# Gates of the dense token tiles by scatter-add into a zeroed table, and an expert product split four and four

## The reference, cut to what matters

```python
s = einsum('thpd,hpnd->thpn', (ht @ w_q).reshape(T, 8, 2, 128), sub_keys)
vals, idx = top_k(s, 16)                       # per head, per half
cand = vals[:, :, 0, :, None] + vals[:, :, 1, None, :]
top_s, top_pos = top_k(cand.reshape(T, 8, 256), 16)
experts = i1 * 128 + i2                        # 8 heads x 16 = 128 experts a token, of 16384
gates = softmax(top_s)                         # over the 16 of a head
a = gelu(einsum('td,ted->te', x, u_tab[experts]))
y = einsum('te,ted->td', gates * a, v_tab[experts])
x = x + gate2 * rmsnorm(y)
```

## Time and profile before

| what | us |
|---|---|
| time, median of 3 runs (lowest to highest) | 2855.0 (2849.57 to 2856.36) |
| span of the profiled execution, first to last instruction | 2847.3 |
| TensorE matmul busy in it | 2774.5 (97%) |
| VectorE busy | 2158.4 (76%) |
| ScalarE busy | 1249.3 (44%) |
| GpSimd busy | 1313.3 (46%) |

### The profile page before, as it was taken

One profiled execution on the slowest core, in us unless ns is written; L12 is line 12 of the kernel. 1 busy time (PEld: TensorE's weight loads), 2 busy tenths in 40 slices (PEclk: granted clock), 3 DMA queues, 4 the chain that ended last, 5 costly groups with the idle time before them and its releaser, 6 DMA issues.

```text
span 2847.3 us, 43522 instructions
## 1 busy us (share of the span) xinstructions
PE 2774.5 (97%) x15948; PEld 2538.1 (89%) x15948; DVE 2158.4 (76%) x3708; ACT 1249.3 (44%) x2302; POOL 1313.3 (46%) x1036
## 2 busy tenths in 40 slices
PE   6998999999999999999999999999999999999998
PEld 5776778889999999999999999999998887877786
DVE  7655545887668778678989898777768878887888
ACT  4333662233357767744454544445522233332233
POOL 0002000000000000177878887777778888888884
PEclk9998999999999999999999999999999999999999
DMA  7520223225556566589898999899999999999996
GB/s 281 227 71 31 89 75 111 69 78 177 182 177 211 200 203 205 185 286 316 301 329 301 314 303 331 308 331 311 321 361 380 359 333 345 374 341 356 341 358 262
DMA packets 328417, 721.37 MB, mean 253 GB/s; under 512 B 44000, under 2 KB 159840, under 8 KB 326368
## 3 DMA queue, kind: packets, MB, share of 16 engines
q1 hardware_dynamic: 238176, 451.18, 44.9%
q0 software_dynamic: 90112, 268.76, 27.3%
HBM read 605.50 MB, written 114.30 MB: 253 GB/s over the span
## 4 chain that ended last, share of the span: by engine, by line
PE 57%; POOL 18%; issue 5%; DVE 2%; ACT 1%; DMA 1%; DVEq 0%; SPq 0%; ACTq 0%; POOLq 0%
PE mix L1434 47%; POOL picked_act L1872 9%; POOL rows L1879 9%; PE mix L116 5%; PE sps_all L1929 2%; PE sps_all L1947 1%; PE mix L1947 1%; ACT onehot L1641 1%; PE sps_all L1521 1%; DMA rows<-in_v,eidx 0%; DVE lo L106 0%; DVE onehot L1723 0%; DMA wq_raw<-in_w_q 0%; DVEq L1123 0%; ACT hi L101 0%
## 5 line engine op out<-in xcount | busy, mean ns | idle before, releaser
L1872 POOL DMA_INDIRECT picked_act<-act_early,aidx x384 | 467.0, 1216 | 1043.0 <-PE mix L1434 938.5
L1434 PE MATMUL mix<-a_hi,hi 128*128 128x320 f32 (+1 forms) x3072 | 810.1, 318 | 2.0 <-DVE lo L106 1.9
L1434 PE MATMUL mix<-a_lo,hi 128*128 128x320 f32 (+1 forms) x3072 | 808.8, 317 | 0.0
L1434 PE MATMUL mix<-a_hi,lo 128*128 128x320 f32 (+1 forms) x3072 | 808.5, 317 | 0.0
L1879 POOL DMA_INDIRECT rows<-in_v,eidx x512 | 651.3, 1272 | 166.4 <-issue 133.2
L1782 DVE SCALAR_TENSOR_TENSOR ys<-rows,coef,ys 128x1024 f32<-128x1024 f32 x504 | 633.9, 1284 | 118.6 <-DMA rows<-in_v,eidx 105.3
L106 DVE TENSOR_TENSOR lo<-raw,hi 128x1024 fp32r<-128x1024 f32 x384 | 469.2, 1222 | 301.4 <-ACT hi L101 301.0
L101 ACT ACTIVATE hi<-raw 128x1024 fp32r<-128x1024 f32 x384 | 404.8, 1054 | 358.3 <-PE mix L1947 348.3
L1434 PEld LDWEIGHTS mix<-a_hi,hi 128*128 128x128 f32 x3072 | 533.6, 188 | 3.2 <-ACT gelu L1650 2.3
L1434 PEld LDWEIGHTS mix<-a_lo,hi 128*128 128x128 f32 x3072 | 535.1, 188 | 0.0
L1434 PEld LDWEIGHTS mix<-a_hi,lo 128*128 128x128 f32 x3072 | 534.7, 188 | 0.0
(11 more groups left out here) (268 smaller groups left out, 3899.3 us busy)
## 6 DMA issues: line engine op xcount, KB each, us to landing
raw<-in_u SPq DMA_DIRECT2D x256, 512.0 KB, 4.9
raw<-in_v SPq DMA_DIRECT2D x128, 512.0 KB, 6.0
act_late<-gelu SPq DMA_DIRECT2D x128, 320.0 KB, 4.6
act_in<-act_late SPq DMA_DIRECT2D x128, 256.0 KB, 6.5
act_early<-gelu SPq DMA_DIRECT2D x128, 192.0 KB, 1.8
gate_d<-free_lo SPq DMA_DIRECT2D x19, 1024.0 KB, 8.1
gt<-gate_d SPq DMA_DIRECT2D x64, 256.0 KB
free_lo<-gate_d SPq DMA_DIRECT2D x64, 256.0 KB, 7.6
```

The lines of the kernel that those rows point to most:

```text
L1434: done = pe.matmul(dst, w, a[:, k, cols], start=first, stop=last)
L1872: pool.indirect_dma_start(out=g.picked_act[:, e:e + 1], out_offset=None, in_=act_tables[e // (EARLY * CHOSEN)], in_offset=bass.IndirectOff ...
```

## The change

It has two halves that lean on each other.

**Gates by scatter-add.** The gate products with everything around them go (`gate_turn` to `key_rounds`, `take_slots`, `compare`, `weigh`, `gates`, `load_gates`). In their place stands one table in DRAM, `act_gates` [128 steps, 128, 512 activations + 512 gates]. SP zeroes its gate half with eight DMAs of 4 MB in the retrieval. GpSimd, before its gathers, issues 4 tiles x 128 indirect DMAs that each add 128 gates to their places; a tile's next head waits until the 16 of its last head have landed. The dense stage loads activations and gates of a step with one DMA.

**Four and four.** `EARLY` becomes 4. The tiles are swapped: tiles 0 to 3 are dense, tiles 4 to 7 gathered. The first sweep does the four gathered tiles, the second the four dense ones, each with 24 matmuls of 512 columns. Top-k of tiles 0 to 2 is done with the scores, now in groups of two heads; tile 3 comes first in the later top-k, then 4 to 7. Rows still begin at step 133, with 21 in 10 steps, and then 2 a step. The order and number of GpSimd's picks and row fetches is the same.

```diff
-EARLY = 3
+EARLY = 4
+GATHERED_TILES = tuple(LATE + s if s < EARLY else DENSE + s - EARLY for s in range(GATHERED))
-HEAD_TILES = EARLY
+HEAD_TILES = DENSE - 1
-TOPK_ORDER = (1, 2, 3, 4, 0)
+TOPK_ORDER = tuple(t - HEAD_TILES for t in (HEAD_TILES, *GATHERED_TILES))
-ROW_EVERY = (5 / 12, 7 / 12)
+ROW_EVERY = (10 / 21, 1 / 2)
...
-    rows = 12 * (min(m, late) - ROWS_FROM + 1) // 5
-    return min(GATHERED * CHOSEN, rows + max(0, m - late) * 12 // 7)
+    rows = 21 * (min(m, late) - ROWS_FROM + 1) // 10
+    return min(GATHERED * CHOSEN, rows + max(0, m - late) * 2)
...
     if m < N:
-        parts = [(acc[:, 0:EARLY * P], slice(0, EARLY * P))]
+        parts = [(acc[:, 0:EARLY * P], slice(LATE * P, S))]
+    elif LATE * P <= HALF:
+        parts = [(acc[:, 0:LATE * P], slice(0, LATE * P))]
...
+    def clear_gates(j):
+        tables = g.act_gates[j * ZERO_TILES:(j + 1) * ZERO_TILES, :, DTOK:].rearrange("n p c -> p n c")
+        sp.dma_start(tables, g.zeros[:].unsqueeze(1).to_broadcast([P, ZERO_TILES, DTOK])).then_inc(g.zeros_stored, 16)
+
+    sp.wait_ge(g.zeros_ready, 1)
     for n in range(QTILES):
         if n + 2 < QTILES:
             sp.wait_ge(g.wq_lo_ready, n + 1)
             sp.dma_start(g.wq_raw[n % 2][:], i["w_q"][n + 2]).then_inc(g.wq_in[n % 2], 16)
+        if n < N // ZERO_TILES:
+            clear_gates(n)
...
+def finish_heads(g, dve, b):
...
+    dve.wait_ge(g.heads_exps, b + 1)
+    dve.tensor_reduce(norm, gates, AX, ALU.add)
+    for h in range(HEAD_GROUP * b, HEAD_GROUP * (b + 1)):
+        dve.scalar_tensor_tensor(g.sidx[:, 0:HEAD_TILES, h, :], g.chosen_r[:, h, :, :, 1], float(NKEYS), g.chosen_r[:, h, :, :, 0],
+                                 ALU.mult, ALU.add)
+    dve.drain()
+    dve.reciprocal(norm, norm)
+    for c in range(HEAD_TILES):
+        slots = g.sidx[:, c, group_heads(b), :]
+        dve.tensor_scalar(slots, slots, float(AG), g.gate_col[:, c:c + 1], ALU.mult, ALU.add)
+    dve.drain()
+    dve.tensor_tensor(gates, gates, norm.unsqueeze(3).to_broadcast([P, HEAD_TILES, HEAD_GROUP, TOPK]), ALU.mult)\
+       .then_inc(g.scatter_ready, 1)
...
+    def scatter_gates(t, head):
+        if head:
+            pool.wait_ge(g.scattered[t], 16 * TOPK * head)
+        for k in range(TOPK):
+            pool.indirect_dma_start(out=gate_table, out_offset=bass.IndirectOffsetOnAxis(ap=g.sidx[:, t, head, k:k + 1], axis=0),
+                                    in_=g.gates_d[:, t, head, k:k + 1], in_offset=None, compute_op=ALU.add)\
+                .then_inc(g.scattered[t], 16)
+
+    pool.memset(g.zeros[:], 0.0).then_inc(g.zeros_ready, 1)
+    for head in range(HEADS):
+        if head == 0:
+            pool.wait_ge(g.zeros_stored, 16 * N // ZERO_TILES)
+        if head % HEAD_GROUP == 0:
+            pool.wait_ge(g.scatter_ready, head // HEAD_GROUP + 1)
+        for t in range(HEAD_TILES):
+            scatter_gates(t, head)
+    pool.wait_ge(g.scatter_ready, HEADS // HEAD_GROUP + 1)
+    for head in range(HEADS):
+        scatter_gates(HEAD_TILES, head)
     act_complete(N - 1)
...
-        dve.tensor_tensor(pieces(g.cf[n % 2]), gates, pieces(g.act_in[n % ACTS]), ALU.mult)\
-           .then_inc(g.cf_ready, 1)
+        dve.wait_ge(g.ag_in_sem[n % ACTS], 16 * (n // ACTS + 1))
+        both = g.ag_in[n % ACTS]
+        dve.tensor_tensor(g.cf[n % 2][:], both[:, 0:DTOK], both[:, DTOK:], ALU.mult).then_inc(g.cf_ready, 1)
```

More of the change, by code:

```diff
@@ L62 @@
 TOPK_FROM, TOPK_PERIOD = 7, 40
[L65 to L73, removed]
+AG = 2 * DTOK
+ZERO_TILES = 16
+DENSE_FROM = 2 * N - 8
 DENSE_ORDER = (2, 3, 0, 1)
-GATE_PIECES = 2
 POOL_ADDS = 2
 ROWS_FROM, PICKS, BEATS = 133, 4, 4
-ROW_EVERY = (5 / 12, 7 / 12)
+ROW_EVERY = (10 / 21, 1 / 2)
 PICKS_FROM, PICKS_AHEAD = N + 0.75, 12
@@ L1227, in token_numbers @@
         dve.tensor_scalar(g.token_col[:, s:s + 1], g.token_col[:, 0:1], float(s % EARLY * P), None, ALU.add)
+    for t in range(DENSE):
+        dve.tensor_scalar(g.gate_col[:, t:t + 1], g.token_col[:, 0:1], float(DTOK + t * P), None, ALU.add)
 def topk_turn(m):
@@ L1233, in topk_turn, with stores_of, acts_stored @@
     return (x, at) if m >= TOPK_FROM and x < TOPK_TILES else (None, None)
[L1236 to L1264, removed]
-def key_step(m):
-    x, batch = gate_turn(m)
-    if m < 2 or (x is not None and (batch < 0 or gate_batch(m) == 0)):
-        return None
-    return m < N, None if x is None else onehot_buffer(gate_batch(m))
-def key_rounds(first):
-    whole = lambda m: [key_step(n) for n in range(m, m + ROUND)]
-    if first + ROUND > 2 * N or None in whole(first):
-        return 0
-    return next(n for n in range(1, 2 * N) if first + (n + 1) * ROUND > 2 * N or whole(first + n * ROUND) != whole(first))
+def stores_of(m):
+    return 1 if m < N or LATE == DENSE else 2
+def acts_stored(last, s):
+    return 16 * sum(stores_of(m) for m in range(s, last + 1, GELUS))
 def rows_by(m):
@@ L1385, in load_raw, with load_act_gates @@
     sp.dma_start(g.raw[m % RAWS][:], src).then_inc(g.raw_in[m % RAWS], 16)
[L1388 to L1399 removed]
+def load_act_gates(g, sp, n):
+    sp.dma_start(g.ag_in[n % ACTS][:], g.act_gates[n]).then_inc(g.ag_in_sem[n % ACTS], 16)
 def split_expert_hi(g, act, m):
@@ L1548, in gathered_steps @@
             if m == last_row_at(s) + (1 if s < GATHERED - 1 else -3):
+                if s == 0:
+                    for t in range(DENSE):
+                        sp.wait_ge(g.scattered[t], 16 * CHOSEN)
                 if s < GATHERED - 1:
@@ L1823, in sweeps_vector @@
         first_tiles(m)
-        x, batch = gate_turn(m - 1)
-        if x is not None and batch < 0:
-            take_slots(x)
-        elif x is not None:
-            add_gate_low(x * GATE_BATCHES + batch)
-        if gate_batch(m + 2) is not None:
-            compare(gate_batch(m + 2))
         topk_steps(m)
@@ L1953, in dense_product @@
             done.then_inc(g.tile_done, 1)
[L1955 to L1975 removed]
+    expert_product(g, pe, 1)
+    for first, last in ((2, N), (N, 2 * N)):
+        rounds = (last - first) // ROUND
+        with pe.Fori(0, rounds) as q:
+            for m in range(first, first + ROUND):
+                expert_product(g, pe, m, ROUND * q)
+        for m in range(first + rounds * ROUND, last):
+            expert_product(g, pe, m)
     dense_product(0)
```

267 lines of the change are left out of this document (87 added, 180 removed).

## The result

| | us |
|---|---|
| kernel after, median of 4 runs (lowest to highest) | 3124.85 (3120.09 to 3138.28) |
| kernel before, beside it | 2855.68 (2849.57 to 2857.01) |
| ratio, 95% interval | 1.0956 (1.093 to 1.0982) |
| span of the profiled execution after | 3118.3 |
| forecast (range) | 2948 (2815 to 3060) |

The change costs 9.6%. The direction was foreseen; the time lies 65 us above the top of the range.

A forecast was written before the change was run, and what follows sets the result against it. TensorE bounds the start, then GpSimd's gather issues, held up by VectorE: first row at 1343 + 1553 for 1010 instructions + 38.5 tail = 2934.5 us span; 7.7 around it and 6 for scatter risk give 2948 (range 2815 to 3060).

The forecast's parts named there:

- The scatters' price: GpSimd before its gathers: an adding scatter costs about a pick, 1.25 us undisturbed, 1.61 at worst, 1.40 taken.
- that margin: Before the first pick: scatters end at 1291 us against the pick's 1326, so they are hidden by 35 us only.
- Rival 2: GpSimd's scatters are late, at 1.6 us or more each or slow landings: 72 us and more, 3010 to 3050; chance 0.22.
- The fourth tile: GpSimd's last 128 scatters: tile ready at 876 us, they add 203 us after 1088 and end at 1291.
- The first sweep: TensorE's early key steps last 5.44 us, not 4.17, so the first pick comes at 1326 and first row near 1343.
- The main case: Gathers start later, scatters are in time, cadence is 1.49 to 1.60 us: 2895 to 3005 us; chance 0.53.
- The cadence: GpSimd's 1010 instructions after the first row: 1.52, 1.42 and 1.60 us each in three stretches, mean 1.538, sum 1553 us.
- Rival 1: GpSimd's gathers in steps 133 to 383 keep their pace and time falls: 2803 us at cadence 1.40; chance 0.20.
- TensorE's savings: Key steps and gate batches: 42 us from wider matmuls and 61 us from gate products, about 103 us for TensorE alone.
- Zeros: Eight DMAs of 4.19 MB in the retrieval, 12.6 us each, landed about 550: effect taken as 0, allowed 0 to 15 us.
- the sign that was named: A retrieval that ends after 640 us would mean that the DMAs writing zeros are in the way.
- Around the span: Outside the profiled execution: 7.7 us lie between the profiled span and the median run time.

The follow-up runs named there:

- Run 1: The changed kernel with all 512 scatters as plain writes instead of adds: 3508.91 us, ratio 1.2127 to the kernel before.
- s384: The changed kernel without the 128 scatters of tile 3, the other 384 adding as before: 2958.13 us, ratio 1.0204 to the kernel before.
- s0: The changed kernel with all 512 scatters left out, zeros still written: 2962.26 us, ratio 1.0211 to the kernel before.
- run 9: The changed kernel itself, unaltered, measured again on another chip: 3146.91 us, ratio 1.0914 to the kernel before.
- Run 10: As s0, but the sums of the first 256 rows lie in PSUM: 2934.57 us, ratio 1.017 to the kernel before.
- Runs 5: As s0, but VectorE adds only 8 of 1024 columns of every odd row: 2926.09 us, ratio 1.0112 to the kernel before.
- 11: As s0, but from the third row of a tile on, each adds only 8 columns: 2944.56 us, ratio 1.0204 to the kernel before.
- run 12: As Run 10, but with four gelu buffers instead of three: 2947.68 us, ratio 1.0172 to the kernel before.

## Why the prediction was wrong, point by point

**The scatters' price: the step that failed.** "For GpSimd's time the nearest is a pick: 1.25 us undisturbed, 1.61 us at worst" was the bound, and 1.40 was taken. Measured from start to start: 1.85 undisturbed, 1.946 in the mean. Run 1 shows that it is the add: the same instruction without it is issued in 0.96 us. The bound from above was made of hold-ups on a form that wasn't the form in question, so it bounded nothing. By the measured price the prediction's own sum comes out: 541.3 + 512 × 1.946 = 1537.7 for the first pick instead of 1326, 13 picks of 1.25 us later the first row at 1553.9 (measured 1553.71), and then 1010 × 1.538 + 38.5 gives 3146; the span was 3118.3. The prediction's own line "each 0.1 us costs 51 us once that margin is used" was right. With 0.55 us above the 1.40 it was the largest uncertainty by far, and the range gave it 72 us.

**Rival 2** had the mechanism, the signature ("if its first pick comes well after 1326") and what waits behind it. Its size, 3010 to 3050, is too small for the same reason, and of its two causes the first was right. Landings were not slow: 13.2 us of waiting in all.

**The fourth tile.** The prediction put its 128 scatters behind the other 384 (1088 + 203 = 1291), and that was right: in the trace GpSimd never idles between 541 and 1536 for more than its gaps and 13.2 us of landings, where the sum had 24. It is one line of work, the fourth tile's first scatter starts at 1282.2, and that the tile is ready at 876 plays no part.

**The first sweep.** Steps of 5.44 us, no gate matmuls, TensorE 600.0 of 600 us busy; where the sweep and not the scatters releases it, the first pick comes at 1339.7 and 1340.5 (s384, s0), forecast 1326; the 14 us are told under the zeros. The main case (loss of start time by moving a tile into the first sweep) holds by itself: forecast 2942 of 2855, 1.030; measured 1.021 in s0. The ratio agrees better than its terms, which is in part luck: in s0 the first row is 16 us late and the cadence 1.564, and the kernel before ran 47 us slower on that chip too.

**The cadence.** Forecast 1.52, 1.42 and 1.60, mean 1.538; measured in the changed kernel 1.46, 1.43 and 1.59, mean 1.516: 22 us too much. The order of the three stretches and the fall in each were right; why the first fell further than forecast wasn't tested. The same kernel on another chip (run 9) has 1.543, so a miss of this size is within what chips differ by. Its cause held: in the dense stage the timelines of GpSimd and VectorE of after show the same pattern as the earlier trace rows.

```profile
2604.09 1.36 POOL L1812 DMA_INDIRECT picked_act<-act_early,aidx  x1 [0.30 <-issue]
2605.75 1.27 POOL L1819 DMA_INDIRECT rows<-in_v,eidx  x1 [0.30 <-issue]
2607.33 1.43 POOL L1812 DMA_INDIRECT picked_act<-act_early,aidx  x1 [0.30 <-issue]
2609.06 0.94 POOL L1819 DMA_INDIRECT rows<-in_v,eidx  x1 [0.30 <-issue]
```

```profile
2604.92 1.28 DVE L1731 SCALAR_TENSOR_TENSOR ys<-rows,coef,ys 128x1024 f32<-128x1024 f32 x1 [0.29 <-DMA rows<-in_v,eidx]
2606.12 0.68 DVE L1754 TENSOR_TENSOR cf<-ag_in 128x512 f32<-128x512 f32 x1
2606.73 1.22 DVE L102 TENSOR_TENSOR lo<-raw,hi 128x1024 fp32r<-128x1024 f32 x1
2607.86 0.68 DVE L102 TENSOR_TENSOR c_lo<-cf,c_hi 128x512 fp32r<-128x512 f32 x1
2608.46 0.16 DVE L1722 TENSOR_TENSOR coef<-picked_act,picked_gates 128x8 f32<-128x8 f32 x1
```

The pick of 2607.33 starts while a split's operation runs, which gives way to the next at 2607.86, and lasts until 2608.76, 0.90 us after that, as in before; the row fetch of 2609.06 finds VectorE idle (the next sum starts at 2609.93) and takes 0.94. Run 10 moved one operand to PSUM and the mean issue fell to 1.033: for the row sum that is shown by experiment, for the split and the product (`tensor_tensor`) it rests on timelines like this one. The Trainium skill, "SBUF — State Buffer", section "Who interferes with whom", says that `tensor_tensor` did not stall DMAs, and infers as the reason that it takes only the read interface of the shared ports. For these indirect DMAs the measurements say otherwise: 1.43 us for the pick beside the split against 0.94, and for the two-input row sum 1.185 against 1.033.

**Rival 1** (faster, cadence below 1.451) needs a faster issue. Runs 5, 10 and 11 gave it one, down to 1.03 us, and the ratio stayed between 1.011 and 1.020. So the fast case wasn't near even with that hold-up mostly gone; what stops it next is open (run 12).

**TensorE's savings.** The products went as foreseen (15948 to 12352), but the busy time fell by 35.8 us, not by 103, since those behind the standstill take 0.237 us and not 0.2267. It was worth nothing either way, since GpSimd sets the end.

**Zeros.** Eight DMAs landed in 17.8 us in the median, not 12.6, and the first scatter waited for them until 541.3, forecast 550. (The prediction's own rows give 12.1 for one.) The 0 that was taken for their effect was wrong, inside the 0 to 15 us that were allowed. The 631.0 of the prediction is step 1 reckoned back from step 5; the first key product, step 0, starts at 622.0 before and at 632.5 after. ScalarE's split waits 72.8 us for query weights from 430 to 632 us, before 4.5, and the last products of the retrieval end at 640.0, before at 628.2: just the sign that was named. With VectorE's work for the last heads TensorE has its even pace only from step 3 on, at 655.1 in s0, which puts step 1 at 644.2 by the same reckoning, 13 us late. In the changed kernel this hides behind the scatters; in s0 and s384 it is in the first pick.

**Around the span** lie 6.6 us (3124.85 − 3118.3), for 7.7.

## What to carry to other kernels

An engine that issues DMAs one by one is a serial resource with a price for each form; a form that stands in no row has no upper bound from its neighbours, and with 512 of them the range must be made of that doubt (0.1 us was 51 us here). Before moving work onto an engine that looks idle, add up its line to the moment at which others first need it: 384 scatters were free here, the next 128 cost about 200 us. Where a hold-up is found on an issue, removing it only pays down to the next limit, and a run that takes it out fully (here the sum in 8 columns) shows cheaply that there is one.

## What the runs showed of the hardware

- An indirect DMA of 128 values of 4 bytes from SBUF to DRAM is issued in 0.96 us plain and 1.55 us with an add; a fetch of 128 rows of 4 KB in 0.94. The bytes don't matter to the issue, the accumulation does. The adding form is also made of more packets: the software queue has 163840 in the changed kernel and 106496 in plain, 112 fewer for each of the 512 scatters.
- Plain 4-byte writes at one in 1.26 us nearly stopped the core's other transfers (6 GB/s in one 100 us stretch) and TensorE (31 of 100 us busy). With a wait for each landing, 2.68 us apart, there was no such effect, and none with the adding form at 1.85. That plain writes in quick succession did it is shown; whether by their number under way or their rate, and where it jams, is not.
- TensorE's granted clock was 1.00 (2.4 GHz) in the full first sweep, and in the standstill from 1340 to 1530 us, with 38.57 us of work in 190, it fell to a mean of 0.61, between 2.4 and 1.2 GHz; it was 0.98 again in the stretch from 1600 us.
- In the retrieval, with the zeros going out, the core moved 400 GB/s from 434 to 541 us, above the 358 that the prediction had from the Trainium skill, "DMA: Bandwidth & Descriptors", section "Specifications". That row works its figure out as half of what a memory stack gives, the share of one of two cores; as a limit of this core it isn't borne out.
